# A triangular solve by 32-row blocks, two groups of heads a stage apart, inside a one-core transformer kernel

## The chip, the cores and the metric

The kernel runs on one core of a Trainium2 chip. The metric is the device time of one execution in microseconds (us). PE is TensorE, PEld its weight loads, DVE is VectorE, ACT ScalarE, POOL GpSimd, SP SyncE; a name with a q behind it is that engine's queue of instructions or DMA issues.

## The reference, cut to what matters

The program is a chain of blocks on 256 tokens of width 1024: a recurrent mixer (RWKV-7), a convolutional feed-forward, latent attention with a feed-forward, and a second block (attention beside a state-space model) with a third feed-forward. All is float32. The change is in the first mixer, and in how the three feed-forwards lay out their input.

```python
def _rwkv7_step(S, inp):
    r, w, k, v, a, b = inp
    sa = jnp.einsum('bhvk,bhk->bhv', S, a)
    S = S * w[:, :, None, :] + sa[..., None] * b[:, :, None, :] + v[..., None] * k[:, :, None, :]
    y = jnp.einsum('bhvk,bhk->bhv', S, r)
    return S, y
...
    _, y = lax.scan(_rwkv7_step, S0, seq)
    mean = jnp.mean(y, axis=-1, keepdims=True)
    var = jnp.mean(jnp.square(y - mean), axis=-1, keepdims=True)
    yn = ((y - mean) * lax.rsqrt(var + LNX_EPS)).reshape(B, T, D) * lnx_w + lnx_b
    bonus = (jnp.sum(rh * kh * r_k, axis=-1, keepdims=True) * vh).reshape(B, T, D)
    out = ((yn + bonus) * g).astype(x.dtype)
    return out @ w_o
```

There are 16 heads of 64, so v is 256 tokens x 16 heads x 64. The feed-forward multiplies the normed input (256 x 1024) with w_in (1024 x 5632), runs a causal convolution of three taps over half of it, and multiplies with w_out.

## The kernel before, in words

**The scan as matrices.** The 256 tokens are two tiles a = 0, 1 of 128. Within a tile the recurrence of a head is a unit lower triangular system of 128 rows with 64 right sides: (I - N) u = rhs. `n_off` (buffers W_N) holds N^T without its 32x32 blocks on the diagonal, `z` (W_Z) the block-diagonal matrix of the inverses of those blocks, which DVE works out by itself earlier. `steps(b)` on PE multiplies n_off by z, four heads to a bank, and ACT writes the result over n_off (line 1603). A sweep then is u <- rhs + n_off^T u; since n_off has four block rows, three sweeps reach the end (`SWEEPS` = NB - 1 = 3), and a fourth product with the second copy of z (loaded from y_dram by `rwkv_inverse_late_sp`) gives u.

**The order on PE** (`rwkv_pe`, second half) is written by hand, and each engine runs its own list strictly in order; between engines there are counting semaphores. A group is 8 heads, g = 0, 1. `key_values(g)` makes the part of rhs that comes from v and the keys (4 calls for two tiles of two groups); DVE's `centred_values` takes it out of the bank and subtracts each head's mean. `sweep(a, s)` has 8 heads for g = 0 and then 8 for g = 1; DVE's `summed(a, s)` adds rhs to the bank (line 1805) and writes `sums`, on which the next sweep waits (`sum_ready`). For tile 0, steps 4 to 7 and key_values(2), (3) stand between the sweeps; for tile 1 y_values and y_state. `y_values(a, q)` multiplies the masked reads with the centred values, `y_solved(a, q)` adds the part of u and closes the bank, `y_state(q)` adds the state's part for tile 1. Between tiles, a loop over 16 heads (lines 1433, 1434) makes the state, DVE scales it into s1 (1846), PE multiplies it with the removal keys (1441), and DVE adds that to rhs of tile 1 (`state_added`, 1811).

**Column halves.** key_values, sweep, y_values and y_solved go through `by_columns` (line 295): the 128x128 stationary tile is cut into two tiles of 64 columns, and there are two matmuls, one to each half of the bank's partitions. All of these are fp32 with 64 moving columns per head, and an fp32 matmul shows as two loads and two matmul records.

**What follows y.** ACT squares the bank (`squares`, 1623), DVE sums and adds the epsilon (`variance`, 1772 and 1773), POOL takes the root (`pow`, 1918), DVE scales, gates and adds the rest (`gated_out`, 1779, 1781, 1783), PE turns the result (`o_turn`, 1399), ACT and DVE split it into a high and a low part (`o_evac` 1627, `o_lo` 1788). "rest" is lnx_b plus bonus times v, made by DVE (`bonus_added`, 16 small operations of line 1823), and gated by POOL (1912, 1914). ACT's `centred` (1611) subtracts each head's mean from v itself, in place, 16 small operations for a tile.

**The projection.** `wide_rows` with w_o: 8 steps (a, s), two tiles by 4 slots of weights, each of 12 products of fp32r with 512 moving columns (lines 282 to 284), and `o_tiles` ahead of each step. Weights are split for that: ACT copies the high part (`split_act`, 407), DVE subtracts (`split_dve`, 413); `ahead(engine, n, ...)` emits these splits up to ring slot n, so their place in each engine's list is set by where the call stands. The ring has 4 slots; SP's list of DMAs (`weights_sp`) waits for a slot to be free, for y_dram to be saved and for z to be cleared, in order. After the projection come the norms of `ffn_front_dve` and the feed-forward.

**The feed-forward.** `ffn_pe` gets its input as a high and a low part, `FFN_H` and `FFN_H_LO`, in two buffers of the arena (12 and 10, then twice 0 and 5). For each weight tile `product_twice` (lines 288, 289) multiplies the high weights with both parts at once, 512 moving columns that `beside(i, j)` takes as two pieces of 256 from two buffers, and the low weights with the high part, 256 columns. `early` makes the first tiles of the next feed-forward before its norms are through; their raw weights are loaded by `early_in(f, p)` on SP, into EARLY_RAW.

Of the kernel before, what the change touches and what calls it, by code (L numbers as in the profile page):

```python
# [27 lines left out]
F32 = mybir.dt.float32  # L28
# [127 lines left out]
def build(nc, A, const_dram, out):  # L156

    with ExitStack() as ctx:
# [99 lines left out]
        XN_FFN0 = 11  # L258
# [183 lines left out]
        def turn_act(act, turn, a, base, hi):  # L442

            for q in range(2):
                act.wait_ge(turned, half_turns(turn, a) * 2 + q + 1)
                nc.scalar.activation(chan(hi, arena12)[:, 4 * q:4 * q + 4, a * P:(a + 1) * P],
# [3 lines left out]
        def turn_dve(dve, turn, a, base, hi, lo=None, parts=(0, 1)):  # L450

            for q in parts:
# [3 lines left out]
                nc.vector.tensor_tensor(chan(lo, arena12)[at], src, chan(hi, arena12)[at].bitcast(F32),  # L456
# [212 lines left out]
        def ffn_front_act(act, f, i, turn, last):  # L669

            hi = FFN_H[f]
# [16 lines left out]
        def ffn_front_dve(dve, f, i, turn, last):  # L688
            hi, lo, xn = FFN_H[f], FFN_H_LO[f], XN if f else XN_FFN0
# [29 lines left out]
        FFN_H, FFN_H_LO, FFN_F, FFN_F_LO, FFN_CONV, FFN_P = (12, 0, 0), (10, 5, 5), 1, 6, 4, 9  # L719
# [23 lines left out]
        EARLY_RAW, EARLY_HI_AT = ((0, 8), (3, 7), (7, 12)), ((7, 1), (2, 8), (8, 2))  # L743
# [40 lines left out]
        def ffn_pe(pe, f, i, turn):  # L784

            first = FIRST[f"ffn_in{f}"]
            h2, h_parts = chan2(FFN_H[f], FFN_H_LO[f]), beside(FFN_H[f], FFN_H_LO[f])
# [29 lines left out]
            def tile(it, j):  # L817
# [9 lines left out]
                for g in range(2):  # L827
                    if isinstance(it, int) and it == j == 0 and g == 1:
                        early_turn(1, 1)
                    for k in range(DC):  # L830
                        mm = product_twice(bank[pair + g], both(w, slice(None), k, g), h2[0][:, k], h_parts[:, :, k],
                                           k == 0, k == DC - 1)
# [191 lines left out]
        def start_dve(dve):  # L1024
# [27 lines left out]
            for g, row in enumerate((3, 4)):  # L1052
# [28 lines left out]
        W_RHS, W_SUM0, W_SUM1, W_U0 = 4, 0, 7, 1  # L1081
# [8 lines left out]
        sums, u = [buf(W_SUM0, 0, D), buf(W_SUM1, 0, D)], [buf(W_U0, 0, D), buf(W_SUM1, D, 2 * D)]  # L1090
        s1 = buf(W_U0, D, 2 * D).rearrange("p (c n) -> p c n", n=P)
        rest = [buf(W_QUERY).rearrange("p (c t) -> p c t", t=T)[:, :, 0:P],
                buf(W_LNX, D, 2 * D).rearrange("p (c t) -> p c t", t=P)]
        mid, last_e, s_scale = small(16), small(8), small(8)
# [15 lines left out]
         sweep_mm, sum_ready, u_out, rem_mm, state_mm, state_ready, ymm, lnx_landed, rest_read, s1_zeroed, c_ready,  # L1110
# [3 lines left out]
                             "state_mm", "state_ready", "y_mm", "lnx_landed", "rest_read", "s1_zeroed", "c_ready",  # L1114
# [11 lines left out]
        SWEEPS = NB - 1  # L1126
        STEP_BANKS = 2 * NT * H // 8
        sweeps_before = lambda a, s: 2 * ((SWEEPS + 1) * a + s - 1)
        sums_before = lambda a, s: 2 * ((SWEEPS + 1) * a + s - 1)

# [18 lines left out]
        def rwkv_pe(pe):  # L1149
# [209 lines left out]
            def sweep(a, s):  # L1359

                last = s == SWEEPS + 1
                if last:
                    pe.wait_ge(z_landed, (NT + a + 1) * 16 * NB)
# [2173 lines left out]
```

## Time and profile before

| What | us |
| --- | --- |
| Median of three runs | 1096.93 (1094.85 to 1100.52) |
| The profiled execution | 1099.76 |
| Its span | 1097.9 |
| PE busy | 1071.0 (98%) |
| DVE busy | 801.8 (73%) |
| ACT busy | 605.1 (55%) |
| POOL busy | 209.3 (19%) |
| Mean granted clock | 0.997 of 2.4 GHz |

The span is the time between the first and the last instruction in the profile; the 1.9 us beside it lie around them. A line of the timeline is: start, time until the last of the merged instructions ended, engine, line of the kernel, operation, what is written and read with its shape, how many records, and in brackets the idle time ahead of it and what ended it ("issue": nothing that the profile shows). For matmuls "128*64 128x64" is the stationary tile and the moving one. Matmuls are pipelined: a record lasts some 0.2 to 0.4 us while the next begins much earlier, so the spacing of starts is what counts. PEclk is the granted TensorE clock, 1.00 being 2.4 GHz and 0.50 being 1.2.

### The profile page before, as it was taken

How to read it: one execution, taken by the hardware profiler on the slowest of the kernel's cores; microseconds unless marked ns; L12 is line 12 of the kernel's file. 1: busy time of each engine (PE TensorE's matmuls, PEld its weight loads, DVE VectorE, ACT ScalarE, POOL GpSimd, SP SyncE). 2: the span in 40 equal slices, each digit the busy share in tenths (PEclk: the TensorE clock that was granted, in tenths of full speed). 3: DMA queues.
4: the chain of work that ended last, by engine and by line, in shares of the span. 5: the costliest groups of instructions: out<-in, count | busy, mean ns of one | idle time of the engine just before them, and what ended most of it. 6: DMA issues, size and time to landing. Idle time of an engine off the chain costs nothing.

```text
span 1097.9 us, 19100 instructions
## 1 busy us (share of the span) xinstructions
PE 1071.0 (98%) x7335; PEld 924.8 (84%) x7335; DVE 801.8 (73%) x1134; ACT 605.1 (55%) x928; POOL 209.3 (19%) x230
## 2 busy tenths in 40 slices
PE   7999989999999999999999999999999999999997
PEld 6997788888888889789888888998777789888886
DVE  7997887778885758777788746688867776655543
ACT  6765354556664566856566544635665445545532
POOL 0134552112221011001222200470100001122200
PEclk9999999999999999999999999999999999999999
DMA  8553181646666566345667575456452654666552
GB/s 250 170 170 115 46 262 43 172 116 192 185 189 228 196 148 161 118 130 146 188 188 194 174 286 158 155 192 213 148 140 83 194 166 131 184 189 191 192 191 77
DMA packets 219748, 183.13 MB, mean 167 GB/s; under 512 B 43265, under 2 KB 197614, under 8 KB 219678
## 3 DMA queue, kind: packets, MB, share of 16 engines
q1 hardware_dynamic: 215710, 171.43, 52.1%
q0 software_dynamic: 3392, 8.66, 2.5%
q10 hardware_dynamic: 576, 2.07, 0.5%
q8 instruction: 49, 0.80, 0.3%
q14 instruction: 21, 0.17, 0.1%
HBM read 179.44 MB, written 2.69 MB: 166 GB/s over the span
## 4 chain that ended last, share of the span: by engine, by line
PE 82%; DVE 12%; issue 2%; ACT 1%; POOL 1%; DMA 1%; SPq 0%; DVEq 0%; POOLq 0%; ACTq 0%
PE bank L288 21%; PE bank L282 13%; PE bank L284 13%; PE bank L283 13%; PE bank L289 10%; PE bank L295 3%; DVE ring L413 3%; PE bank L1238 2%; DVE arena L1655 1%; DVE arena L1750 1%; DVE stat L1748 1%; PE bank L371 1%; PE bank L2123 1%; PE bank L1353 1%; DVE arena L1680 0%
## 5 line engine op out<-in xcount | busy, mean ns | idle before, releaser
L413 DVE TENSOR_TENSOR ring<-ring,arena 128x2048 fp32r<-128x2048 f32 (+1 forms) x138 | 312.3, 2266 | 113.0 <-ACT arena L407 111.4
L282 PE MATMUL bank<-arena 128*128 128x512 f32 (+3 forms) x980 | 343.8, 351 | 2.0 <-DVE ring L413 1.6
L288 PE MATMUL bank<-arena 128*128 128x512 f32 x960 | 339.8, 399 | 0.0
L407 ACT ACTIVATE arena<-ring 128x2048 fp32r<-128x2048 f32 (+1 forms) x145 | 272.0, 1879 | 93.0 <-DMA ring<-in_ffn_w_out 43.2
L289 PE MATMUL bank<-arena,ring 128*128 128x256 f32 x960 | 269.6, 281 | 0.0
L284 PE MATMUL bank<-arena 128*128 128x512 f32 (+3 forms) x720 | 264.9, 368 | 0.0
L288 PEld LDWEIGHTS bank<-arena 128*128 128x128 f32 x960 | 180.4, 188 | 44.7
L283 PE MATMUL bank<-ring,arena 128*128 128x512 f32 (+2 forms) x560 | 216.2, 386 | 0.0
L282 PEld LDWEIGHTS bank<-arena 128*128 128x128 f32 x980 | 185.5, 189 | 27.1 <-issue 3.7
L289 PEld LDWEIGHTS bank<-arena,ring 128*128 128x128 f32 x960 | 181.5, 189 | 0.0
L284 PEld LDWEIGHTS bank<-arena 128*128 128x128 f32 x720 | 135.6, 188 | 22.3
L283 PE MATMUL bank<-arena 128*128 128x256 f32 (+3 forms) x420 | 122.1, 291 | 0.0
L283 PEld LDWEIGHTS bank<-ring,arena 128*128 128x128 f32 x560 | 105.3, 188 | 19.9
L880 ACT ACTIVATE arena<-bank 128x256 f32<-128x256 f32 x60 | 23.0, 383 | 122.2 <-PE bank L289 122.2
L283 PEld LDWEIGHTS bank<-arena 128*128 128x128 f32 x420 | 80.3, 191 | 1.1
L961 POOL CAST arena<-arena 128x256 f32 (+1 forms) x60 | 27.0, 450 | 260.1 <-DVE arena L916 260.1
L284 PE MATMUL bank<-arena,ring 128*128 128x256 f32 x260 | 73.5, 283 | 0.0
L923 DVE TENSOR_TENSOR arena<-bank,arena 128x256 f32<-128x256 f32 x120 | 45.4, 419 | 33.3 <-ACT arena L880 33.2
L935 DVE SCALAR_TENSOR_TENSOR arena<-arena,cols 128x255 f32<-128x255 f32 x80 | 50.8, 635 | 9.5 <-ACT arena L886 0.8
L523 POOL TENSOR_TENSOR stat<-stat 128x1 f32<-128x1 f32 x12 | 6.6, 553 | 263.5 <-DVE stat L518 263.5
L295 PEld LDWEIGHTS bank<-arena 128*64 128x64 f32 x1344 | 43.0, 141 | 9.8 <-issue 5.4
L284 PEld LDWEIGHTS bank<-arena,ring 128*128 128x128 f32 x260 | 49.8, 192 | 0.0
(335 smaller groups left out, 1282.7 us busy)
## 6 DMA issues: line engine op xcount, KB each, us to landing
ring<-in_ffn_w_in SPq DMA_DIRECT2D x80, 512.0 KB, 5.1
ring<-in_ffn_w_out SPq DMA_DIRECT2D x44, 512.0 KB, 4.4
ring<-in_w_gate_up SPq DMA_DIRECT2D x40, 512.0 KB, 5.1
ring<-in_w_in SPq DMA_DIRECT2D x18, 1024.0 KB, 5.0
ring<-in_a_w_rkv SPq DMA_DIRECT2D x12, 1024.0 KB, 5.5
ring<-in_w_down SPq DMA_DIRECT2D x22, 512.0 KB, 3.7
ring<-in_a_w_o SPq DMA_DIRECT2D x4, 1024.0 KB, 8.4
arena<-in_ffn_w_in SPq DMA_DIRECT2D x8, 512.0 KB, 4.7
```

What stands on the lines that cost most here:

```text
L282: nc.tensor.matmul(dst, stationary[0], moving[0], start=start, stop=False)
L283: nc.tensor.matmul(dst, stationary[0], moving[1], start=False, stop=False)
L284: return nc.tensor.matmul(dst, stationary[1], moving[0], start=False, stop=stop)
L288: nc.tensor.matmul(dst[:, :], stationary[0], both_parts, start=start, stop=False)
L289: return nc.tensor.matmul(dst[:, 0:T], stationary[1], hi, start=False, stop=stop)
L295: mm = nc.tensor.matmul(dst[cells], stationary[:, cells], moving, start=start, stop=stop)
L407: nc.scalar.activation(buf(hi_of(n), 0, w, arena12), ring[:, r, 0:w], ACT.Copy).then_inc(hi_ready, 1)
L413: on.tensor_tensor(ring12[:, r, 0:w], ring[:, r, 0:w], buf(hi_of(n), 0, w, arena12).bitcast(F32), ALU.subtract).then_inc(split_ready, 1)
L880: nc.scalar.activation(whole_sum[0][j % 2], bank[pair][:, T:2 * T], ACT.Copy).then_inc(act_done, 1)
L923: nc.vector.tensor_tensor(whole_sum[g][j % 2], bank[pair + g][:, 0:T], whole_sum[g][j % 2], ALU.add).then_inc(conv_step, 1)
L935: nc.vector.scalar_tensor_tensor(conv[:, back:T], gate[:, 0:T - back], conv_at(f, it, j, tap[i]), conv[:, back:T], ALU.mult, ALU.add).then ...
L961: nc.gpsimd.tensor_copy(tile_cells(fT_hi, it, j), gated[seat(j)]).then_inc(ffn_hi, 1)
```

## The change

- **The solve works in place by blocks of 32 rows.** A part (g, b) multiplies, for the 8 heads of group g, only the 32 columns of block b of n_off (a stationary tile of 128x32) with rhs, into 32 partitions of the bank; DVE's `block_added` adds these 32 rows into rhs itself. The blocks follow each other, and the two groups of heads are a stage apart: (0,1); (0,2) with (1,1); (0,3) with (1,2); (1,3). In a pair the heads of the two groups alternate. `sums` is gone; the last product with z reads rhs, per group (`block_inverses`).
- **steps** makes and ACT copies 96 instead of 128 columns a head.
- **One matmul a head** with a 128x128 stationary tile instead of two halves in key_values, block_inverses, y_values and y_solved. Other users of by_columns stay.
- **Centred values** go to a buffer of their own, one POOL operation a tile (`values_centred`), instead of 16 of ACT; the value times the bonus is made by ACT (`bonus_scaled`, 16 small operations a tile), and the shift is added by POOL, instead of DVE's bonus_added.
- **The order** on PE, ACT, DVE, POOL and SP is rewritten around it, as the diff shows. On SP the first block of w_o is loaded ahead of z's second copy, early_in(0,0) waits for ymm 2 and c_ready 4, early_in(2,1) for attn_gated 4 instead of yn_ready and the slots of attn_proj.
- **The feed-forward's input** is in two adjacent buffers, with the high and the low 256 columns of a channel chunk next to each other, so product_twice reads 512 columns in a row (`FFN_H` = 11, 10, 11; `XN_FFN0` 10; one EARLY_RAW seat 5).

```diff
-        def beside(i, j):
-            i, j = sorted((i, j))
-            return arena12[0][:, i:j + 1:j - i, :].rearrange("p s (c t) -> p s c t", t=T)
+        def beside(i):
+            return bufs(i, 2, arena12).rearrange("p (c x t) -> p c x t", x=2, t=T)
...
-        FFN_H, FFN_H_LO, FFN_F, FFN_F_LO, FFN_CONV, FFN_P = (12, 0, 0), (10, 5, 5), 1, 6, 4, 9
+        FFN_H, FFN_F, FFN_F_LO, FFN_CONV, FFN_P = (11, 10, 11), 1, 6, 4, 9
...
-                    mm = by_columns(bank[g][:, i * N:(i + 1) * N], lk[g // 2][:, h, :], v[:, g // 2, h * N:(h + 1) * N],
-                                    True, True)
+                    mm = nc.tensor.matmul(bank[g][:, i * N:(i + 1) * N], lk[g // 2][:, h, :], v[:, g // 2, h * N:(h + 1) * N],
+                                          start=True, stop=True)
...
+            def block_sweep(a, parts):
+                for g, b in parts:
+                    if b > 1:
+                        pe.wait_ge(sum_ready, SUM_NO[a][g, b - 1])
+                    elif a == 0:
                         pe.wait_ge(u_rhs, g + 1)
+                        pe.wait_ge(step_in, 2 * (g + 1))
                     else:
+                        pe.wait_ge(sum_ready, STATE_ADDED + g + 1)
+                        pe.wait_ge(step_in, STEP_BANKS)
+                for i in range(8):
+                    for g, b in parts:
+                        h, cells = 8 * g + i, rows_of_block(b)
+                        mm = nc.tensor.matmul(bank[g][cells, i * N:(i + 1) * N], n_off[a][:, h, cells],
+                                              rhs[a][:, h * N:(h + 1) * N], start=True, stop=True)
+                        if i == 7:
+                            mm.then_inc(sweep_mm, 1)
...
-            sweep(0, 1)
+            block_sweep(0, ((0, 1),))
             steps(4)
+            block_sweep(0, ((0, 2), (1, 1)))
             steps(5)
-            sweep(0, 2)
             steps(6)
+            block_sweep(0, ((0, 3), (1, 2)))
             steps(7)
-            sweep(0, 3)
             key_values(2)
-            sweep(0, SWEEPS + 1)
+            block_sweep(0, ((1, 3),))
+            block_inverses(0, 0)
             key_values(3)
+            block_inverses(0, 1)
...
             y_values(0, 0)
-            y_values(0, 1)
...
             y_solved(0, 0)
-            y_solved(0, 1)
+            y_values(0, 1)
...
+            y_solved(0, 1)
+            block_sweep(1, ((0, 1),))
...
             y_values(1, 0)
+            block_sweep(1, ((0, 2), (1, 1)))
             y_values(1, 1)
-            sweep(1, 1)
             y_state(0)
-            sweep(1, 2)
+            block_sweep(1, ((0, 3), (1, 2)))
             y_state(1)
-            sweep(1, 3)
-            sweep(1, SWEEPS + 1)
+            block_sweep(1, ((1, 3),))
+            block_inverses(1, 0)
             o_turn(0, 0)
-            o_turn(0, 1)
+            block_inverses(1, 1)
             for q in range(2):
                 pe.wait_ge(u_out, 2 + q + 1)
                 y_solved(1, q)
+            o_turn(0, 1)
...
                 elif (a, s) == (0, 2):
-                    o_turn(1, 0)
                     pe.wait_ge(o_split, 2)
                 elif (a, s) == (0, 3):
-                    o_turn(1, 1)
+                    o_turn(1, 0)
                 elif (a, s) == (1, 0):
                     pe.wait_ge(o_split, 3)
+                elif (a, s) == (1, 1):
+                    o_turn(1, 1)
...
+            def block_added(a, g, b):
+                rows, cells = rows_of_block(b), slice(g * HALF, (g + 1) * HALF)
+                dve.wait_ge(sweep_mm, SOLVED * a + SWEEP_NO[g, b])
+                nc.vector.tensor_tensor(rhs[a][rows, cells], bank[g][rows, :], rhs[a][rows, cells], ALU.add).then_inc(sum_ready, 1)
...
+            state_added(0)
+            state_added(1)
             variance(0, 0)
-            state_added(0)
+            block_added(1, 0, 1)
             variance(0, 1)
-            state_added(1)
+            block_added(1, 0, 2)
+            block_added(1, 1, 1)
             gated_out(0, 0)
-            summed(1, 1)
+            block_added(1, 0, 3)
+            block_added(1, 1, 2)
+            block_added(1, 1, 3)
             gated_out(0, 1)
-            summed(1, 2)
+            o_lo(0, 0)
             ahead(dve, FIRST["w_o"] + 1, split_dve)
-            summed(1, 3)
-            o_lo(0, 0)
             o_lo(0, 1)
             ahead(dve, FIRST["w_o"] + 2, split_dve)
             variance(1, 0)
             variance(1, 1)
             gated_out(1, 0)
             ahead(dve, LAST["w_o"], split_dve)
+            o_lo(1, 0)
             gated_out(1, 1)
-            o_lo(1, 0)
             early_lo(dve, 0, 0)
             o_lo(1, 1)
...
+            values_centred(0)
+            values_centred(1)
+            pool.wait_ge(lnx_landed, 32)
+            rest_gated(0)
+            rstd(0)
+            rstd(1)
+            rest_gated(1)
+            rstd(2)
+            rstd(3)
...
             rwkv_inverse_sp(sp)
+            rows_of("w_o", A["a_w_o"][0], 2, range(0, 1))
             rwkv_inverse_late_sp(sp, 0)
-            rows_of("w_o", A["a_w_o"][0], 2, range(0, 2))
+            rows_of("w_o", A["a_w_o"][0], 2, range(1, 2))
             rwkv_inverse_late_sp(sp, 1)
             rows_of("w_o", A["a_w_o"][0], 2, range(2, 4))
-            sp.wait_ge(sweep_mm, sweeps_before(0, SWEEPS + 1) + 2)
+            sp.wait_ge(ymm, 2)
+            sp.wait_ge(c_ready, 4)
             early_in(0, 0, A["ffn_w_in"][0])
```

## Rows read from the trace of the kernel before

**Rows 1.** The page, sections 1 (busy time) and 5 (a group: busy, mean ns, idle).
```profile
PE 1071.0 (98%) x7335; PEld 924.8 (84%) x7335; DVE 801.8 (73%) x1134; ACT 605.1 (55%) x928; POOL 209.3 (19%) x230
...
L288 PE MATMUL bank<-arena 128*128 128x512 f32 x960 | 339.8, 399 | 0.0
```

**Rows 2.** Waits of PE from 126 to 215: us, times, longest.
```profile
PE bank L1433 <- issue: 2.6, 1, 2.6
...
PE bank L295 <- issue: 1.7, 1, 1.7
PE bank L1399 <- DVE arena L1783: 1.6, 2, 0.9
PE bank L295 <- DVE arena L1805: 0.7, 1, 0.7
```

**Rows 3.** Timeline of PE.
```profile
134.32 2.08 PE L295 MATMUL bank<-arena 128*64 128x64 f32 x64
...
162.57 3.28 PE L295 MATMUL bank<-arena 128*64 128x64 f32 x63
...
178.64 2.08 PE L295 MATMUL bank<-arena 128*64 128x64 f32 x64 [0.72 <-DVE arena L1805]
...
183.69 0.50 PE L282 MATMUL bank<-arena 128*128 128x512 f32 x1
```

**Rows 4.** Busy time of PE, PEld, DVE, ACT, POOL by stretch, clock, DMA.
```profile
153.50:155.20 1.70, 0.02 (x2) 0.02 (x2) 1.67 (x5) 1.70 (x2) 1.07 (x1) 1.00 0.50 74
...
159.10:161.70 2.60, 0.03 (x1) 0.00 (x0) 1.98 (x1) 0.79 (x4) 0.00 (x0) 1.00 1.02 384
161.70:165.20 3.50, 3.46 (x66) 3.46 (x68) 1.41 (x3) 0.60 (x1) 0.00 (x0) 0.52 1.04 269
```

**Rows 5.** Timeline of the weight loads (PEld), two windows.
```profile
134.32 1.95 PEld L295 LDWEIGHTS bank<-arena 128*64 128x64 f32 x64 [0.33 <-issue]
...
142.11 1.86 PEld L1353 LDWEIGHTS bank<-arena 128*128 128x128 f32 x16
...
763.17 0.97 PEld L2647 LDWEIGHTS bank<-arena,cst 128*128 128x128 f32 x8
```

**Rows 6.** Timeline of SP's queue: DMA issues.
```profile
137.23 0.34 SPq L1946 DMA_DIRECT2D y_blocks<-arena  x1
143.83 1.90 SPq L1934 DMA_DIRECT2D arena<-y_blocks  x4
...
155.23 30.46 SPq L3273 DMA_DIRECT2D arena<-in_ffn_w_in  x4
```

**Rows 7.** Timeline of DVE.
```profile
149.29 0.69 DVE L1805 TENSOR_TENSOR arena<-bank,arena 128x512 f32<-128x512 f32 x1 [2.04 <-PE bank L295]
...
150.84 3.21 DVE L1823 SCALAR_TENSOR_TENSOR arena<-arena,stat 128x64 f32<-128x64 f32 x16
...
157.23 3.85 DVE L413 TENSOR_TENSOR ring<-ring,arena 128x2048 fp32r<-128x2048 f32 x1
...
175.61 2.28 DVE L413 TENSOR_TENSOR ring<-ring,arena 128x2048 fp32r<-128x2048 f32 x1
```

**Rows 8.** Timelines of ACT and POOL.
```profile
148.69 3.92 ACT L1611 ACTIVATE arena<-arena,stat 128x64 f32<-128x64 f32 x16
...
156.56 2.37 POOL L1914 TENSOR_TENSOR arena<-arena 128x1024 f32<-128x1024 f32 x1
```

**Rows 9.** PE by stretch: busy time (records), clock, DMA.
```profile
230.00:330.00 100.00, 100.00 (x567) 1.00 0.67 189
340.00:395.00 55.00, 55.00 (x245) 1.00 0.53 194
702.00:732.00 30.00, 30.00 (x252) 1.00 0.48 149
```

**Rows 10.** Timeline of PE, two windows.
```profile
81.44 1.14 PE L1238 MATMUL bank<-arena 64*128 64x256 f32 x8
...
764.26 1.13 PE L2663 MATMUL bank<-arena 64*128 64x256 f32 x8
```

More of the change, by code:

```diff
@@ L450, in turn_dve @@
         def turn_dve(dve, turn, a, base, hi, lo=None, parts=(0, 1)):
+            hi, lo = (chan(x, arena12) if isinstance(x, int) else x for x in (hi, lo))
             for q in parts:
@@ L830, in tile @@
                     for k in range(DC):
-                        mm = product_twice(bank[pair + g], both(w, slice(None), k, g), h2[0][:, k], h_parts[:, :, k],
+                        mm = product_twice(bank[pair + g], both(w, slice(None), k, g), h2[0][:, k], h_parts[:, k],
                                            k == 0, k == DC - 1)
@@ L1089, in build @@
         rhs = [buf(W_RHS, D, 2 * D), buf(W_RHS, 0, D)]
-        sums, u = [buf(W_SUM0, 0, D), buf(W_SUM1, 0, D)], [buf(W_U0, 0, D), buf(W_SUM1, D, 2 * D)]
+        centred = [buf(m, 0, D) for m in W_LK]
+        u = [buf(W_U0, 0, D), buf(W_LK[1], D, 2 * D)]
         s1 = buf(W_U0, D, 2 * D).rearrange("p (c n) -> p c n", n=P)
@@ L1379, in y_values, with block_inverses @@
+            def block_inverses(a, g):
+                pe.wait_ge(z_landed, (NT + a + 1) * 16 * NB)
+                pe.wait_ge(sum_ready, SUM_NO[a][g, NB - 1])
+                for i in range(8):
+                    h = 8 * g + i
+                    mm = nc.tensor.matmul(bank[(0, 4)[a] + g][:, i * N:(i + 1) * N], z[a][:, h, :], rhs[a][:, h * N:(h + 1) * N],
+                                          start=True, stop=True)
+                mm.then_inc(sweep_mm, 1)
             def y_values(a, q):
@@ L1907, in rwkv_pool, with values_centred, rest_gated, rstd @@
             nc.gpsimd.memset(buf(W_U0, D, 2 * D), 0.0).then_inc(s1_zeroed, 1)
-            pool.wait_ge(lnx_landed, 32)
-            for a in range(NT):
-                g = toks(W_G)[:, a, :]
-                pool.wait_ge(rest_read, a + 1)
-                nc.gpsimd.tensor_tensor(rest[a], rest[a], g.rearrange("p (c t) -> p c t", t=P), ALU.mult).then_inc(c_ready, 1)
-                pool.wait_ge(c_ready, 2 * a + 1)
+            def values_centred(a):
+                pool.wait_ge(means_ready, a + 1)
+                pool.wait_ge(u_mm, 2 * (a + 1))
+                cells = lambda m: m.rearrange("p (h n) -> p h n", n=N)
+                nc.gpsimd.tensor_tensor(cells(centred[a]), cells(toks(W_V)[:, a, :]),
+                                        spread(v_mean[:, a * H:(a + 1) * H].unsqueeze(2), [P, H, N]), ALU.add).then_inc(v_evac, 1)
+            def rest_gated(a):
+                g = toks(W_G)[:, a, :]
+                chunks = lambda m: m.rearrange("p (c t) -> p c t", t=P)
+                pool.wait_ge(bonus_copied, NT + a + 1)
+                nc.gpsimd.tensor_tensor(rest[a], bonus[a], chunks(buf(W_LNX, D, 2 * D)), ALU.add).then_inc(c_ready, 1)
+                pool.wait_ge(c_ready, 3 * a + 1)
+                nc.gpsimd.tensor_tensor(rest[a], rest[a], chunks(g), ALU.mult).then_inc(c_ready, 1)
+                pool.wait_ge(c_ready, 3 * a + 2)
                 nc.gpsimd.tensor_tensor(g, g, buf(W_LNX, 0, D), ALU.mult).then_inc(c_ready, 1)
-            for j in range(2 * NT):
+            def rstd(j):
                 stat = slice(8 * j, 8 * (j + 1))
```

152 lines of the change are left out of this document (69 added, 83 removed).

## The prediction

> **What bounds the kernel now.** I read the page's engine table first: TensorE (PE) is busy for 1071.0 of 1097.9 us, VectorE (DVE) for 801.8 [rows 1]. So PE time counts one for one, and the other engines count only where PE waits for them. The waits of PE around the solve come second [rows 2]: two with the releaser "issue", 2.6 and 1.7 us, and one of 0.7 us for a sum of DVE. Third, PE's own timeline [rows 3] from the first key products at 134.32 to the first product of the output projection at 183.69, 49.4 us, in which PE otherwise runs without a break. A view by stretches [rows 4] explains the two "issue" waits: at 153.5 and at 159.1 PE does almost nothing while the DMA engines are at 0.50 and 1.02 of their share, everything that PE needs by semaphore is long done, and the second wait falls in the middle of a loop. I read them as PE waiting for its own instruction stream, which comes by DMA (argued, no row names it). In the stretch after the second wait the granted clock is 0.52, that is 1.2 GHz instead of 2.4 for most of it. Its products (y_solved and the rest of the state loop) took 3.28 us for 63 records where 64 take 2.08 elsewhere [rows 3]: 1.3 us more with the tail of the loop.
>
> **One matmul instead of two column halves.** An fp32 matmul leaves two records. By halves, 64 records (32 half matmuls, two groups of 8 heads) load in 1.95 us and take 2.08 with the last one's end, so 1.01 us for a group of 8 heads, 31.5 ns a record [rows 5, 3]. The change has 16 records per group, each with a stationary tile of 128x128. No row has that tile with 64 moving columns, but two rows enclose it [rows 5]: with 16 moving columns 8 loads take 0.97 us, less the last one's 0.19 over 7 steps is 111 ns; with 128 moving columns 16 loads take 1.86 us, again 111 ns. The step doesn't depend on the moving columns, so the load sets it, and the two ends of the bound are the same value: 16 x 0.111 = 1.78 us per group. It touches key_values (4 groups), the inverses (4), y_values (4) and y_solved (4): 16 x (1.78 - 1.01) = **+12.3 us** of PE. The Trainium skill ("TensorE: Matmul & The Clock Gate", section Back-to-back issue gap) gives a sustained spacing of about 81 ns for pairs of load and matmul at 128 columns. By that figure a group would be 1.30 us and this term +4.6; the trace disagrees, at 111 ns.
>
> **Sweeps by 32-row blocks.** Before, a sweep is 2 groups of 1.01 us, three sweeps for each of 2 token tiles: 12.1 us. After, a tile has (0,1), (0,2)+(1,1), (0,3)+(1,2), (1,3). A pair alternates between two column groups of the array as the halves do: 32 records, 1.0 us. A single part stays in one column group; one half of the old scheme gave a record every 63 ns, so 16 records are 1.0 us. (Bounds: 0.5 if records of one column group overlap as well as alternating ones, 1.78 if they step like full loads; I take 1.0, the row with the nearest tile.) Four times 1.0 less switching overlap, 3.9 us a tile, 7.9 in all: **-4.2 us**. steps writes 96 instead of 128 columns but keeps the 111 ns load: 0.
>
> **Instruction stream.** The full-array groups issue half as many instructions over nearly twice the time, so PE eats them at about a third of the rate. The loads of ffn_w_in, which ran from 155.23 beside the second wait [rows 6], move behind ymm 2 and c_ready 4, to about 175. I take both waits and the clock loss as gone: -4.3 - 1.3 = **-5.6 us**; if they stay, 0. The Trainium skill ("TensorE: Matmul & The Clock Gate", section The HAM clock gate) says that activity releases the throttle; the fall after a gap of 2.6 us agrees.
>
> **DVE and the chain of the solve.** block_added has the 512 free elements of summed, on 32 partitions: I price it like L1805, 0.69 us [rows 7] (0.2 to 0.9), 6 a tile as before. bonus_added, 2 x 3.21 us, leaves DVE, where it stood between sums. Placing the new order by these prices: in tile 0 steps and key_values cover each sum, PE gets to (0,3)+(1,2) at 146.5 with the sum there at 146.3. In tile 1 the 0.7 us wait at 178.64 goes (-0.7), but (1,3) waits about 0.6 for block_added(1,2) and small ones add 0.2: **+0.1** together.
>
> **ACT, POOL and the queues.** ACT loses centred (2 x 3.9 us) and gains bonus_scaled (32 small ops, the same 0.245 each) [rows 8]: 0, covered, since solutions keeps its place behind one split. POOL gains four tensor_tensor of 1024 elements (centring and the sum with the shift), 2.37 each [rows 8]: 19 us where it had 9.5. values_centred(0) ends near 144.5 and is wanted at 156; rest_gated(0) ends near 166. But rest_gated(1) is queued behind rstd(1), so it runs from about 173 to 180, over gated_out(0,0) on DVE. There is a row for what that does: the split at 157.23 took 3.85 us beside POOL's L1914 and 2.28 elsewhere [rows 7, 8]. L1781 and L1783 read SBUF twice, as the split does; block_added(1,0,3), and with it the chain to (1,3), is queued behind them. Bounds 0 and 4.7 (two POOL ops); I take **+1.5**. The Trainium skill ("SBUF — State Buffer", section Who interferes with whom) has this as an exclusive lock between a GpSimd op that reads SBUF and a DVE op with two SBUF inputs; the row agrees. SP: the block of w_o that now goes ahead of the z blocks delays them. y_saved took 6.6 us to land (137.23 to 143.83) with little before it [rows 6]; z of tile 0 now comes at about 150, wanted at 151. No cost, 2 us if the block takes long. early_in(0,0) is wanted by ACT at about 189 and lands by 181: 0. The later start of early_in(2,1) on attn_gated stays ahead of its queue's wait for ring slots: 0.
>
> **The tail of the projection.** By halves the last y_solved ended at 183.7; mine ends at about 186.6, and o_turn(0,1) stands behind it, so squares(1,0) on ACT is queued behind o_evac(0,1). DVE then does o_lo(0,1), the split of w_o slot 2, variance, rstd, gated_out(1,0) and the split of slot 3, 2.28 us. That ends 11 us after the last y_solved; PE wants slot 3 after 9.3. And post_scale is queued behind o_lo(1,1), which now waits for o_turn(1,1) at tile (1,1). I count new waits of 0.5, 1.7 and 1.7 us, where the kernel has 1.6 now [rows 2]: **+2.3 us** (0 to 5).
>
> **The FFN input's layout.** product_twice reads 2x256 columns from two buffers 2 or 5 apart; after the change 512 in a row. A pair L288 + L289 takes 100 us / 282.5 = 0.354 us (the count less the two records already running). Contiguous 512 alone steps at 55 / 243.3 = 0.226, contiguous 256 alone at 30 / 249.6 = 0.120, together 0.346 [rows 9]. The page has 960 pairs [rows 1]: up to 960 x 0.008 = 7 us, if the gap is due to the two pieces. Against that, an fp32 matmul with two pieces of 128 in distant buffers takes the same as one with 256 in a row, 8 records in 1.14 and 1.13 us [rows 10]; the gap may lie in the alternation of lengths, which stays. Between ends 0 and -7 with one row for each, I take the middle: **-3.5 us**.
>
> **Sum.** 12.3 - 4.2 - 5.6 + 0.1 + 1.5 + 2.3 - 3.5 = **+2.9 us**. The profiled execution took 1099.8 us with a span of 1097.9, the three runs have a median of 1096.9, 2.8 lower; I carry the difference over: **1099.8 us**. A measurement of this kernel can tell about 0.5%, 5.5 us, from no change.
>
> **The rivals.**
> A: as above, no change that can be told. Chance 0.40.
> B, slower: the instruction waits stay, since the block sweeps still run at full record rate in the same DMA traffic. It speaks for it that loads of 1 MB go out at 137 and 175 beside them; against it that the full-array groups leave time to catch up. Price 5.6 us, 1105.4. It decides as soon as a stretch of the stage shows PE idle with "issue" and a clock below 1. Chance 0.14.
> C, slower: the late chain. Gated outputs blocked by POOL for 4.7 us, and the tail at its bound of 5: +3.2 + 2.7, 1105.7. Chance 0.16.
> D, faster: a 128x128 load followed by another doesn't hold 64-column matmuls to 111 ns but lets them run at 63, as a half does. Then the 12.3 us are 0 and the time 1087.5. Two rows speak against it [rows 5]. At the skill's 81 ns it would be 1092.1. Chance 0.08.
> E, faster: the layout is worth the full 7 us and the tail's new waits are covered: -3.5 - 2.3, 1094.0; with good cover for POOL's lock 1092.5. Chance 0.17.
> F: the layout is worth nothing and the rest as forecast, 1103.3. Chance 0.05.
>
> **How the numbers follow.** Faster by over 0.5% is below 1091.4: D, and a third of E with slack in single prices, 0.16. Slower is above 1102.4: B, C, F and the upper edge of A, 0.36. The rest is 0.48. The ends of my bounds are 1092.5 less slack and 1113; leaving out half of D below and a tenth above gives 1090 to 1108. A alone has 1096 to 1103.
>
> **What would show it.** In the profile after: the key, inverse and read products with 16 records a group and loads 111 ns apart, a block sweep in 1.0 us, no "issue" wait over 1 us and a clock of 1.0 from 134 on; rows L288 and L289 at 0.346 to 0.354 a pair; the first product of the projection near 188, the last near 216. I would be wrong if the full-array groups take 1.0 us, or if the stage ends earlier than now.

## The result, and the profile after

| What | before | after |
| --- | --- | --- |
| Median of four, both kernels on one chip | 1098.43 (1094.85 to 1100.52, 4) | 1110.58 (1109.19 to 1112.01, 4) |
| The profiled execution, its span | 1099.76, 1097.9 | 1110.29, 1108.5 |
| First product L288 of the feed-forward, us from the start of the span | 223.5 | 237.5 |

The ratio is 1.0130, 95% interval 1.0104 to 1.0156: slower by 12 us, where I had forecast +2.9 and a range up to 1108. Of the 14.0 us that the first feed-forward starts later, 11.3 were there at the first product of the projection (195.02; before 183.69 [rows 3]) and 2.7 came in the projection; behind it 3.4 were won back, 14.0 to 10.6 at the end of the span.

The timeline of PE after, with the groups that answer to [rows 3]:
```profile
133.77 3.79 PE L1356 MATMUL bank<-arena 128*128 128x64 f32 x32
...
150.34 1.08 PE L1382 MATMUL bank<-arena 128*32 128x64 f32 x16
151.35 2.00 PE L1392 MATMUL bank<-arena 128*128 128x64 f32 x16
...
170.93 1.09 PE L1382 MATMUL bank<-arena 128*32 128x64 f32 x32
171.95 2.00 PE L1399 MATMUL bank<-arena 128*128 128x64 f32 x16
...
179.59 1.08 PE L1382 MATMUL bank<-arena 128*32 128x64 f32 x16 [2.58 <-DVE arena L1834]
180.60 2.93 PE L1392 MATMUL bank<-arena 128*128 128x64 f32 x16
...
187.48 7.04 PE L1409 MATMUL bank<-arena 128*128 128x64 f32 x32
...
195.02 0.78 PE L282 MATMUL bank<-arena 128*128 128x512 f32 x1
```
Start to start a full-array group takes 1.8 to 1.85 us (L1356: half of 3.62), a block sweep 1.01, single or as a pair: as priced. But behind the sweep at 179.59 the groups slow down: block_inverses(1,0) takes 2.72 us, and y_solved(1,*) 6.83 us for two groups instead of 3.6.

Busy time of PE, PEld, DVE, ACT, POOL by stretch, then granted clock, DMA share and GB/s, after:
```profile
165.00:175.00 10.00, 10.00 (x122) 9.56 (x123) 6.54 (x11) 4.43 (x5) 7.60 (x5) 1.00 0.01 2
179.00:182.00 3.00, 2.41 (x26) 2.32 (x27) 1.80 (x3) 0.00 (x0) 1.29 (x1) 0.91 0.43 105
182.00:185.00 3.00, 3.00 (x17) 3.00 (x16) 1.51 (x3) 0.60 (x1) 0.00 (x0) 0.50 0.00 0
...
181.40:198.50 17.10, 17.10 (x75) 16.41 (x75) 7.43 (x7) 4.77 (x7) 0.00 (x0) 0.50 0.16 46
```
The last row is the miss: 17.1 us at a clock of 0.50, that is 1.2 GHz, while PE is busy 17.10 of 17.10 us. Before, the fall in this stage lasted about 3.4 us [rows 4]. It is not one profile's accident: the mean clock of the four executions of after is 0.990 to 0.992.

The waits of PE from 126 to 226, after (us, times, longest), answer to [rows 2]:
```profile
PE bank L1382 <- DVE arena L1834: 2.9, 2, 2.6
PE bank L375 <- DVE arena L566: 2.0, 1, 2.0
```
No "issue" is left, as forecast. What ended the wait of 2.6 us stands in the timelines of DVE and POOL, after:
```profile
172.05 1.40 DVE L1834 TENSOR_TENSOR arena<-bank,arena 32x512 f32<-32x512 f32 x2 [1.33 <-PE bank L1382]
...
174.21 1.10 DVE L1811 TENSOR_TENSOR arena<-arena 128x512 f32<-128x512 f32 x1
175.35 2.74 DVE L1813 TENSOR_TENSOR arena<-arena 128x512 f32<-128x512 f32 x1
178.12 1.42 DVE L1834 TENSOR_TENSOR arena<-bank,arena 32x512 f32<-32x512 f32 x2
```
```profile
172.41 2.35 POOL L1944 TENSOR_TENSOR arena<-arena 128x1024 f32<-128x1024 f32 x1
174.84 2.69 POOL L1946 TENSOR_TENSOR arena<-arena 128x1024 f32<-128x1024 f32 x1
```
gated_out(0,0)'s two products with two SBUF inputs take 1.10 and 2.74 us beside POOL's rest_gated(1), 0.69 each elsewhere, and block_added(1,0,3) and (1,1,2) are queued behind them. That is the lock that I had priced at +1.5 us, at 2.6 us.

### The profile page after: what moved, and what is told of

It is laid out like the page before. It is cut to its first block, busy times and chain, and to the rows that moved or that the text cites. A ratio compares the mean times of both kernels' runs of the same rounds, so it can differ in the third digit from the quotient of the medians.

```text
span 1108.5 us, 18180 instructions
## 1 busy us (share of the span) xinstructions
PE 1082.3 (98%) x6887; PEld 937.5 (85%) x6887; DVE 799.8 (72%) x1103; ACT 603.9 (54%) x928; POOL 216.6 (20%) x234
## 4 chain that ended last, share of the span: by engine, by line
PE 81%; DVE 12%; issue 2%; DMA 2%; ACT 1%; POOL 1%; SPq 1%; DVEq 0%; POOLq 0%; ACTq 0%
PE bank L288 20%; PE bank L282 13%; PE bank L284 12%; PE bank L283 12%; PE bank L289 10%; DVE ring L417 3%; PE bank L1250 1%; PE bank L375 1%; DVE arena L1685 1%; DVE arena L1780 1%; DVE stat L1778 1%; PE bank L1409 1%; PE bank L1392 1%; PE bank L295 1%; PE bank L2168 1%
## 5 line engine op out<-in xcount | busy, mean ns | idle before, releaser
L288 PE MATMUL bank<-arena 128*128 128x512 f32 x960 | 335.7, 396 | 0.0
L289 PE MATMUL bank<-arena,ring 128*128 128x256 f32 x960 | 267.4, 279 | 0.0
L288 PEld LDWEIGHTS bank<-arena 128*128 128x128 f32 x960 | 180.3, 188 | 42.5
L289 PEld LDWEIGHTS bank<-arena,ring 128*128 128x128 f32 x960 | 180.8, 188 | 0.0
L970 POOL TENSOR_TENSOR arena<-arena 128x256 f32 (+1 forms) x60 | 45.4, 756 | 9.6 <-POOL arena L968 8.6
```

Source lines behind the costliest of these rows:

```text
L288: nc.tensor.matmul(dst[:, :], stationary[0], both_parts, start=start, stop=False)
L289: return nc.tensor.matmul(dst[:, 0:T], stationary[1], hi, start=False, stop=stop)
L970: nc.gpsimd.tensor_tensor(tile_cells(fT_lo, it, j), gated[seat(j)], tile_cells(fT_hi, it, j).bitcast(F32), ALU.subtract).then_inc(ffn_done, 1)
```

## The experiments

All are the kernel before or after with one edit, or a few where the text says so. Ratios are to the kernel before, run beside it on the same chip.

**1. Halves everywhere.** After, with key_values, block_inverses, y_values and y_solved by column halves again:
```diff
-                mm = nc.tensor.matmul(bank[...], rb[a][:, h, :], u[a][:, h * N:(h + 1) * N],
-                                      start=False, stop=h == 8 * q + 7)
+                mm = by_columns(bank[...], rb[a][:, h, :], u[a][:, h * N:(h + 1) * N],
+                                False, h == 8 * q + 7)
```


> The changed kernel, with the key, inverse and read products (16 groups of 8 heads) again as two column halves each. Theory 1 (a 128x128 stationary tile with 64 moving columns is bound by its load, 111 ns a record, and such products also fail to bring the granted clock back after the 2.6 us wait of PE before part (1,3) of tile 1): the groups fall from 1.8-1.95 to 1.01 us, 12 to 14 us of PE work gone; the wait before (1,3) grows by some 2 us for lack of cover; the clock may fall there but is back within 3 to 4 us instead of 17. Time 1092 to 1097. Rival (the length of the half-clock stretch has nothing to do with the form of the products): the stretch stays near 17 us, time 1098 to 1103.

Measured 1098.12 us, ratio 1.0034 (1.0017 to 1.0051). The waits of PE, halves everywhere:
```profile
PE bank L1382 <- DVE arena L1833: 6.4, 3, 4.4
```
The stretch in which its clock was down (busy times as above, clock, DMA):
```profile
172.30:179.10 6.80, 4.66 (x52) 4.18 (x52) 4.63 (x7) 0.60 (x1) 2.77 (x2) 0.50 0.44 122
```
The slow products are a large part of the loss, but the rest of the change, without them, still doesn't gain: PE now gets to (1,3) earlier and waits 4.4 us for the same sums. The time is above what I expected (1092 to 1097) and just inside the rival's range, but not for the rival's reason: the clock was down for 6.8 us, not 17. I had expected 3 to 4; 2.1 of the 6.8 fall into the wait itself.

**2. The sums first.** After, with DVE's two sums ahead of gated_out(0,0):
```diff
-            gated_out(0, 0)
             block_added(1, 0, 3)
             block_added(1, 1, 2)
+            gated_out(0, 0)
```


> The changed kernel, with one edit on VectorE: in tile 1 the gated output (0,0), whose two operations with two SBUF inputs took 1.10 and 2.74 us beside GpSimd instead of 0.69, stands behind the block sums (0,3) and (1,2) instead of ahead of them. Theory 1 (the wait of 2.6 us before part (1,3) is what lets the clock fall): no wait over 1 us there, granted clock 1.00 from 130 us on, 2 us of wait and 6 to 8 us of half clock gone, time 1100 to 1103. Rival (the clock falls because TensorE's products of that stage, bound by loads, count as too little work, wait or not): the clock falls to 1.2 GHz all the same, time 1107 to 1110.

Measured 1102.57 us, 1.0075 (1.0052 to 1.0098). The wait falls from 2.6 to 0.4 us, yet the time falls by 0.55%, 6.0 us against the ratio of after. The stretches of the kernel with the sums first say why:
```profile
182.00:185.00 3.00, 2.84 (x27) 2.63 (x24) 2.33 (x4) 0.59 (x2) 0.00 (x0) 1.00 0.00 0
185.00:188.00 3.00, 3.00 (x29) 3.00 (x29) 2.48 (x2) 0.49 (x2) 0.00 (x0) 1.00 0.00 0
```
The same products now have a clock of 1.00, and 27 and 29 records in 3 us where after has 17 in its row from 182. The clock did fall once more in this profile, from 213.7 to 217.1, behind a wait of 2.0 us for L566.

**3. The wait stays, PE is kept busy in it.** After, with 12 fp32 products of a constant into an unused bank behind y_state(1):
```diff
             y_state(1)
+            keep_busy(pe, 12, 5)
             block_sweep(1, ((1, 3),))
```


> The changed kernel, with 12 idle fp32 products of 128x128 (24 records, some 2.7 us) into an unused bank between the last y_state and part (1,3) of tile 1; everything else, the late sum on VectorE too, stays. Theory 1: the wait is filled, part (1,3) starts at most 0.3 us later than in the changed kernel, the clock stays at 1.00, and 6 to 8 us go, time 1102 to 1105: this is the price of the half clock by itself. Rival (the late sum itself costs the time, through what is queued behind it): time stays at 1110 to 1111.

Measured 1102.5 us, 1.0082 (1.0059 to 1.0104). The timeline of PE, kept busy:
```profile
177.18 2.84 PE L389 MATMUL bank<-cst 128*128 128x128 f32 x24
179.95 1.08 PE L1382 MATMUL bank<-arena 128*32 128x64 f32 x16
...
184.97 3.74 PE L1409 MATMUL bank<-arena 128*128 128x64 f32 x32
...
188.91 0.48 PE L282 MATMUL bank<-arena 128*128 128x512 f32 x1
```
Two of its stretches, the first for all engines, the second for PE alone:
```profile
177.00:195.00 18.00, 18.00 (x143) 16.76 (x142) 12.90 (x15) 6.31 (x8) 4.98 (x3) 1.00 0.41 116
```
```profile
189.00:231.00 42.00, 38.33 (x230) 1.00 0.52 139
```
This separates the wait from the clock. The last block sweep starts at 179.95, 0.36 later than after, so the wait for DVE is paid in full; from there to the projection it takes 8.96 us instead of 15.43. The idle time cost 2.6 us, the clock that fell behind it 6.5 us before the projection, and the whole kernel gains 0.48%, 5.3 us by the ratios (8.1 by the medians of the two kernels; the profiled spans differ by 7.8).

**4. Halves only behind the fall.** After, with halves only in block_inverses(1,*) and y_solved(1,*):
```diff
+                    if a == 1:
+                        mm = by_columns(...)
+                    else:
                         mm = nc.tensor.matmul(...)
...
```


> The changed kernel, with two column halves only in the four groups after the wait: the inverses and read products with u of tile 1. The wait of 2.6 us before them stays. Theory 1 (the form of the products after the wait holds the clock down): the clock falls at about 181 us and is back within 3 to 5 us; 3.4 us of PE work and 5 to 6 us of half clock gone, time 1101 to 1103. Rival (the stretch lasts 17 us whatever runs in it): only the work goes, doubled by the half clock, 5 to 7 us, and the projection's first steps still run at half rate, time 1104 to 1106, with a clock of 0.5 until about 195.

Measured 1101.55 us, 1.0059 (1.0038 to 1.0079). Stretches of PE with the late halves:
```profile
182.00:185.00 3.00, 3.00 (x46) 2.55 (x44) 2.52 (x4) 0.60 (x1) 0.00 (x0) 0.51 0.00 0
185.00:188.00 3.00, 3.00 (x90) 2.93 (x87) 0.88 (x2) 1.08 (x2) 0.00 (x0) 0.92 0.00 0
```
The wait of 2.57 us stays and the clock falls as before, but it is back after 3.4 us. So with the same wait ahead of it the fall was short or long by what ran in it: with the column halves it ended after 3.4 us, with full-array products of 64 columns it lasted until the projection's products with 512 columns had run for 3.5 us (195.0 to 198.5). PE was "busy" in both. That is one profile of each; the mean clocks of all executions agree, 0.992 to 0.998 here (0.992 is the profiled one, where the clock fell a second time, from 199 to 206) and 0.990 to 0.992 in after.

**5. One matmul alone.** Before, with one matmul a head in key_values, the product with z, y_values and y_solved, nothing else:


> The kernel of before with one edit: the key products, the last product with z, and both read products as one matmul a head instead of two halves; the old sweeps, DVE's bonus_added and the old order stay. Theory 1 (the load sets the step, 111 ns a record): 16 groups of 1.01 us become 1.8 to 2.0, 12 to 15 us of PE work more, less up to 5.6 us for the two instruction waits and the clock loss behind them if the slower stream lets them go: time 6 to 15 us over the kernel before. Rival (the products are not bound by loads): within 2 us of before.

Measured 1101.61 us, 1.0059 (1.0032 to 1.0086), +6.5 us; my two terms for it are +12.3 - 5.6 = +6.7. The closeness is partly luck: the medians differ by 5.0 us, and the ten executions are of two kinds, seven with 1099.2 to 1105.5 us and a mean clock of 0.997 to 1.000, three with 1107.9 to 1111.2 and 0.992. A long fall of the clock would do that in the three, but only one execution was profiled, one of the seven. In that profile the projection starts at 190.97, 7.3 us later than before. Its waits of PE from 126 to 226, and one stretch:
```profile
PE bank L1376 <- DVE arena L1810: 0.7, 1, 0.7
PE bank L1404 <- DVE arena L1788: 0.5, 1, 0.5
```
```profile
150.00:155.00 5.00, 5.00 (x92) 4.93 (x92) 3.59 (x14) 4.42 (x17) 2.81 (x2) 1.00 0.96 335
```
The "issue" waits are gone although the DMA share is 0.96; before, it was 0.50 and 1.02 in the two waits [rows 4].

**6 and 7. The layout alone, and the kernel before once more.** Before, with only the feed-forward's layout; and before unchanged.


> The kernel of before with the feed-forward's input laid out as in the changed kernel (high and low 256 columns side by side), and nothing else. Theory 2 (the layout is worth nothing; the pair L288 + L289 has two paces, 354 and 348 ns, and each feed-forward of each run falls into one of them whatever the layout): time within 3 us of before, and the three feed-forwards of the profile may show either pace. Rival (contiguous columns are worth 6 ns a pair): all three at 348 ns, 4 to 6 us faster than before.

> The kernel of before once more, unchanged, for a second profile. Theory 2: the pair L288 + L289 may show 348 ns in one or more feed-forwards, though the columns are in two pieces, and the waits for instructions may stand elsewhere. Rival (two pieces cost 6 ns): 354 ns in all three again.

The layout alone: 1095.89 us, 0.9991 (0.9980 to 1.0003). Before again, one run: 1096.2. PE in a stretch of the third feed-forward (records): before, then after, the layout alone, before again:
```profile
940.00:1020.00 80.00, 80.00 (x455) 1.00 0.67 189
```
```profile
940.00:1020.00 80.00, 80.00 (x464) 1.00 0.70 193
```
```profile
940.00:1020.00 80.00, 80.00 (x464) 1.00 0.66 190
```
```profile
940.00:1020.00 80.00, 80.00 (x464) 1.00 0.66 188
```
A pair L288 + L289 goes at one of two paces: by these rows, less the two records already running, 353 or 346 ns. (From start to start, without the gaps where records are missing, the mean is 353.3 to 353.9 ns in some and 346.6 to 347.0 in the others of the 42 feed-forwards profiled; they are the 354 and 348 of my expectations.) The unchanged kernel reaches the faster one too, in its second profile, in its third feed-forward. So the faster pace doesn't need the layout. With the old layout 9 of 21 feed-forwards ran at it, with the new one 15 of 21: that the layout makes it more frequent is neither shown nor excluded.

**8. Halves and sums first.** After, with the edits of 1 and 2 together.


> The changed kernel with both edits: all 16 groups as column halves, and the two block sums ahead of the gated output on VectorE. Theory 1: the 12 to 14 us of PE work go, and the wait behind the slow gated output goes, though with halves less work stands between the block parts, so 1 to 3 us of short waits remain; the clock stays up from 130 us on, or falls for 3.4 us at most. Time 1 to 5 us under the kernel before (the block sweeps themselves save 4.2). Rival (the block sweeps' chain through VectorE costs more than they save on PE): 2 to 5 us over before.

Measured 1100.22 us, 1.0039 (1.0019 to 1.0058): the rival on record for this run came true. Its waits of PE:
```profile
PE bank L1451 <- issue: 2.6, 1, 2.6
PE bank L1416 <- DVE arena L1812: 2.5, 1, 2.5
PE bank L1382 <- DVE arena L1833: 2.1, 2, 1.7
...
PE bank L282 <- DVE ring L417: 1.5, 1, 1.5
```
The wait for the sums shrinks from 4.4 us at the longest to 1.7, but others stand in its place, and with halves back a wait of kind "issue" is there again (run 1 had none over 0.5 us).

**9 and 10. The loads later.** What is that wait? Before, with ffn_w_in's early load held until the second y_solved (9), and with w_o's last two slots held as well (10). This is 10; in 9 the line with rows_of stays ahead of the new wait:
```diff
-            rows_of("w_o", A["a_w_o"][0], 2, range(2, 4))
-            sp.wait_ge(sweep_mm, sweeps_before(0, SWEEPS + 1) + 2)
+            sp.wait_ge(ymm, 2)
+            rows_of("w_o", A["a_w_o"][0], 2, range(2, 4))
             early_in(0, 0, A["ffn_w_in"][0])
```


> The kernel before, with one edit: the 2 MB load of ffn_w_in (0,0) on SP waits for the second y_solved (about 165) instead of the end of the first solve; the loads of w_o stay. Theory (PE waits for its own instruction stream while the DMA engines are full of weight loads): the wait inside y_solved near 159 to 162, 1.7 to 2.6 us, and the clock's fall after it go, the one at 153.5 stays, since w_o's slots run beside it: -2.5 to -4 us, ratio 0.996 to 0.998. Rival (the wait has its cause in PE's own rate of instructions and the loads only happen to run beside): both waits stay, ratio 1.000, or 1.001 if the later load makes the projection wait.

> As the run before, and the last two slots of w_o wait for the second y_solved too. Theory: the loads beside 153.5 are then those of slots 0 and 1 and of the z blocks alone; the wait there goes or shrinks, and with both gone the time is 4 to 6 us under before, ratio 0.994 to 0.997. Slot 2 of w_o is then split late, at about 170, covered by the second solve: no new wait before the projection. Rival: waits stay where they are, ratio 1.000; or the first slots and z blocks suffice to starve the stream at 153.5 and only the second goes, ratio 0.997.

Measured 1097.03 us, 0.9991 (0.9974 to 1.0009), and 1095.92 us, 0.9995 (0.9978 to 1.0012): no gain, where I had expected 0.996 to 0.998 and 0.994 to 0.997. I had named the wrong load: with the input's alone held, PE still does nothing from 158 to 160, with the DMA share at 1.03. With w_o's last slots held too, that stretch is clean; but 2 us later there is a new wait. Stretches of run 9, then of run 10, then run 10's DVE and wait:
```profile
158.00:160.00 2.00, 0.09 (x3) 0.00 (x0) 2.00 (x1) 0.85 (x4) 1.39 (x1) 1.00 1.03 412
```
```profile
152.00:154.00 2.00, 0.58 (x20) 0.50 (x16) 2.00 (x12) 2.00 (x2) 0.00 (x0) 1.00 0.65 103
...
158.00:160.00 2.00, 2.00 (x68) 1.86 (x63) 2.00 (x1) 1.03 (x3) 1.14 (x1) 1.00 0.04 8
160.00:162.00 2.00, 0.00 (x1) 0.00 (x0) 1.97 (x3) 1.96 (x2) 0.00 (x0) 1.00 0.27 59
```
```profile
156.80 4.49 DVE L413 TENSOR_TENSOR ring<-ring,arena 128x2048 fp32r<-128x2048 f32 x1
161.22 1.40 DVE L1846 TENSOR_TENSOR arena<-bank,stat 64x512 f32<-64x512 f32 x2
```
```profile
PE bank L1441 <- DVE arena L1846: 2.7, 1, 2.7
```
The stall had hidden a late DVE: its split of w_o's first slot, 4.49 us beside POOL, stood ahead of the state's scaling. The clock fell behind the new wait as well, from 163.2 to 166.6.

The trace also says what PE lacked, which I had overlooked: it has a DMA queue of kind "instruction". Queue q8 has 49 transfers of 16 KB in before and 46 in after, and follows PE's number of records (7335 and 6887). The DMA queues of before, 159.2 to 160.3 (packets, MB, share of 16 engines):
```profile
q1 hardware_dynamic: 105, 0.43, 98.0%
q8 instruction: 1, 0.02, 5.6%
```
Before, such transfers land at 153.77 and 160.28, and PE goes on at 155.18 and 161.74, 1.4 and 1.5 us later. All 15 "issue" waits of PE of over 0.5 us in the 14 traces, but for the first 15 us of the program, end in that way, 1.3 to 1.6 us after a transfer of q8 landed. So PE was waiting for its instructions. That the loads held them up is seen beside run 12, with the same list on PE: there the transfer that starts at 152.7 before starts at 150.2, though the stage starts 0.4 us later, and no wait follows.

**11 and 12. A version that beats both.** Run 10 with that split moved behind the second sum of tile 1 and the next one behind the third (11); and with all four slots of w_o and the input's load behind the first y_solved, ACT's split of the first slot behind tile 0's squares (12). This is 11 against 10:
```diff
-            dve.wait_ge(split_ready, SPLIT_NO[LAST["w_v"]] + 1)
-            ahead(dve, FIRST["w_o"], split_dve)
...
             dve.wait_ge(state_mm, 1)
...
             summed(1, 2)
-            ahead(dve, FIRST["w_o"] + 1, split_dve)
+            dve.wait_ge(split_ready, SPLIT_NO[LAST["w_v"]] + 1)
+            ahead(dve, FIRST["w_o"], split_dve)
             summed(1, 3)
+            ahead(dve, FIRST["w_o"] + 1, split_dve)
```


> The kernel before with w_o's last two slots and the input's load behind the second y_solved (as in the run of that name), and DVE's split of w_o's first slot moved from ahead of the state's scaling to behind the sum of the second sweep of tile 1, the split of the second slot behind the third sum. Theory (with the stall of the instruction stream gone, PE's wait of 2.7 us for L1846 was the next limit, 4.5 us of that split standing before it on DVE): the wait falls to 0.5 us or less, the clock stays at 1.00 from 134 to 215, the first pair L288 comes at 218 to 220 where the kernel before has 223.5, ratio 0.995 to 0.997. Rival: another wait takes its place (the sums of tile 1, or the projection's first split), ratio 0.999 to 1.001.

> As the run before, and w_o's first two slots wait for the first y_solved as well, with ACT's split of the first slot behind tile 0's squares. Theory: with no load of weights beside 144 to 160 the wait at 153.5, 1.4 to 2.6 us, goes too, so that no wait of kind issue over 0.5 us is left between 126 and 215: ratio 0.993 to 0.996. Rival 1: the z blocks' loads alone hold the DMA engines at that time and the wait stays, ratio as in the run before. Rival 2: the splits, all late now, make the projection wait, ratio 0.998 to 1.002.

Measured 1090.58 us, 0.9973 (0.9960 to 0.9986), and 1090.86 us, 0.9967 (0.9954 to 0.9981): both faster than either kernel, by 3 to 3.6 us against before; between the two nothing can be told. Both are just above what I expected (0.995 to 0.997 and 0.993 to 0.996). Waits of PE from 126 to 215 of run 11, then of run 12, then a stretch of run 12:
```profile
PE bank L295 <- issue: 2.3, 2, 1.6
```
```profile
PE bank L295 <- issue: 1.1, 2, 0.6
```
```profile
152.00:154.00 2.00, 2.00 (x76) 2.00 (x72) 2.00 (x11) 2.00 (x7) 0.00 (x0) 1.00 0.26 43
```
With no weights loading from 144 to 159 PE runs through at 38 records a microsecond; two waits of up to 0.6 us came up at 168 and 174, where the loads now are. The first product L288 comes at 219.2 and 219.1, where the two profiles of before have 223.5 and 222.0.

**The clock in the kernel before.** A wait doesn't always bring a fall. The second profile of before (run 7) has "issue" waits of 2.4 and 2.3 us in this stage and a full clock, where the first had 1.7 and 2.6 and a fall. Its two waits, and PE from 134 to 215:
```profile
PE bank L295 <- issue: 2.4, 1, 2.4
PE bank L1433 <- issue: 2.3, 1, 2.3
```
```profile
134.00:215.00 81.00, 73.52 (x1224) 1.00 0.57 158
```
So what a wait costs in clock is a matter of the execution in before; in after all four mean clocks are low.

## Why the prediction was wrong

- **The step that failed** is the price of a wait. I gave POOL's lock on gated_out(0,0) +1.5 us, with a bound of 4.7, all of it idle time, and wrote "a clock of 1.0 from 134 on". The lock was where I put it and cost 2.6 us; the clock fell 1.8 us after it, and what stood there were the new slow full-array products. Runs 2 and 3 each take this fall away and win back 6.0 and 5.3 us by the ratios (8.0 and 8.1 by the medians); run 3 leaves the wait in. By the timelines of run 3 and after it is 6.5 us before the projection and 1.6 in its first ten products (4.00 us against 2.36), 8.1 in all, where the sum had nothing; the wait itself was 1.1 us longer than priced. These two add up to the 9.2 us between the forecast of +2.9 and the measured 12.1. The layout, forecast at -3.5, is worth nothing, and the sum comes out even so only because the feed-forwards won back as much by luck (below). In run 3, with its full clock, the projection starts at 188.9, near the 188 that I forecast. I had a fall in [rows 4] and took its length, 3.4 us, as given; that one stood under column halves. The new stream of products was not in the trace of before, and I didn't bound what a fall would cost in it. The rule of the Trainium skill that I cited ("TensorE: Matmul & The Clock Gate", section The HAM clock gate) is about the same gate; I used it only for the waits that go, not for the one that I added.
- **One matmul, +12.3**: right in kind and nearly in size. Groups take 1.8 to 1.85 us against 1.78, some 0.8 us more over 16. The 81 ns that the Trainium skill gives in the section cited in the prediction ("TensorE: Matmul & The Clock Gate", Back-to-back issue gap) would be 1.30 a group by my estimate; the trace disagrees again, at 111 to 116 ns.
- **Block sweeps, -4.2**: 1.01 us each, single or paired, 8.1 in all instead of 12.1, so -4.0: nearly as forecast.
- **The instruction waits, -5.6**: gone in after and in run 5. Run 5 measures this term together with the first: +6.5 against +6.7, with the spread told there. That PE waits for its own instructions was argued in the prediction ("no row names it"); the trace does name it, by the transfers of q8 told behind run 10. Halving the instructions (run 5, DMA share 0.96) or moving the loads (run 12, instructions as before) takes the waits away. What I missed as well is that the second wait hid a late DVE (run 10), so that to remove it alone gains nothing.
- **The layout, -3.5**: worth nothing that can be told, 0.9991 (run 6). In the profile of after the feed-forwards do win back 3.4 us, a number that agrees with my term by luck: two of three ran at the faster of two paces, which the unchanged kernel also has (run 7). The 0.354 us a pair that I read in [rows 9] is the slower pace.
- **The tail, +2.3**: 2.7 in after, of which 1.6 are the half clock of its first ten products. Where the clock is whole all the way (run 3) the first product L288 comes at 231.25, 42.3 us behind the first of the projection, 2.5 more than before's 39.8, with waits of 2.0 for L566 and 1.5 for a split. Right in kind and size.
- **Sum by measured sizes** up to the first product: 13.1 - 4.2 - 5.6 + 2.6 + 0.3 + 6.5 = +12.7, where the profile has +11.3 (0.3 is the wait for a sum at 143.5). Of the 1.4 between, 0.7 is the wait at 178.64 that went, and 0.55 the earlier start of the stage (133.77 against 134.32 [rows 3]).
- **The rivals.** C, the late chain, had the right place, but its price (1105.7) was made of waits alone. No rival had a clock in it.

Open: what sets a feed-forward at 346.7 or 353.3 ns a pair. All three ran at the faster pace in the profiles of 11 and 12, which makes some 6 us of their spans (960 pairs by 6.6 ns); the 2.8 to 4.4 us that they gain up to the first L288 are not of that kind. Open too: when a wait of 2 to 3 us brings the clock down and when not, and why full-array products of 64 columns left it down.

## What to carry to other kernels

Price a wait of some 2 us or more twice: the idle time, and, as a risk, the clock that may fall with or behind it, at the pace of the work that stands behind it. Here the 128x128 products of 64 columns left PE "busy" and the clock down for 17.1 us. Filling the wait with products kept the clock up (run 3), and so did shortening it (run 2); putting such products ahead of the wait would be another way, which no run shows. And before removing a stall look at what was late behind it, and move that in the same step. When PE stands with "issue" as the releaser, look at the DMA queues of kind "instruction" at that time.

## What the runs showed of the hardware that I had not expected

- A fall of the clock lasted 3.4 us under column halves (run 4) and 17.1 under full-array fp32 products with 64 columns (after), both with PE busy all the time. It lasted 6.8 us under halves where 2.1 us of a wait lay in it (run 1), and 6.8 again in run 4 from 199 to 206, with waits of 1.0 and 1.5 us just before and at its start. In before two waits of 2.4 and 2.3 us brought none (run 7).
- PE can lack instructions while its semaphores are all done: 1.4 to 3.4 us at a time, behind stretches with some 34 records a microsecond and a DMA share near 1.0 (before, 150 to 153.5 and 155.2 to 159.1). It goes on 1.3 to 1.6 us after 16 KB on queue q8 have landed. At 18 records a microsecond (run 5), or without weight loads (run 12), it runs through.
- The same feed-forward goes at one of two paces, 1.9% apart, without an edit.
- A DVE product with two SBUF inputs took 2.74 us instead of 0.69 beside a POOL operation on SBUF (after), the split 4.49 instead of 2.28 (run 10).
